# Attention with balanced column halves and inverse sums as repeated stationaries, and a recurrence with whole turnings and products over 128 stacked rows

## What is computed

```python
# attention, per block of 128 queries and head (q and k of 96, v of 64 columns)
s = einsum('bqhd,bkhd->bhqk', q_blk, k) * scale         # masked above the diagonal
o = einsum('bhqk,bkhd->bqhd', softmax(s), v)
# recurrence, per token and head (state S of 64 x 64)
sa = einsum('bhvk,bhk->bhv', S, -kk_t)
S = S * w_t + sa (x) (kk_t * a_t) + v_t (x) k_t
y = einsum('bhvk,bhk->bhv', S, r_t)
```

## Time and profile before

| | us |
|---|---|
| median of 3 runs | 1356.23 (1355.48 to 1357.2) |
| the profiled execution | 1353.33 |
| its span | 1351.5 |
| TensorE busy in the span | 1315.0 (97%) |

### The profile page before, as it was taken

One profiled execution on the slowest core, in us unless ns is written; L12 is line 12 of the kernel. 1 busy time (PEld: TensorE's weight loads), 2 busy tenths in 40 slices (PEclk: granted clock), 3 DMA queues, 4 the chain that ended last, 5 costly groups with the idle time before them and its releaser, 6 DMA issues.

```text
span 1351.5 us, 23894 instructions
## 1 busy us (share of the span) xinstructions
PE 1315.0 (97%) x9900; PEld 1071.2 (79%) x9900; DVE 945.5 (70%) x1110; ACT 474.8 (35%) x796; POOL 497.0 (37%) x323
## 2 busy tenths in 40 slices
PE   7999999999999989989999999999999999999997
PEld 6877677877776789986688878888888888888886
DVE  3657975257777634439677988877777787669877
ACT  3143643146555433334104522212222444333330
POOL 0000112001876210002084778766774354444030
PEclk9999999999999999999999999999999999999999
DMA  5111444779639952224222345444436986666562
GB/s 225 62 48 32 141 157 156 184 169 292 183 101 288 221 127 53 59 64 140 87 101 94 117 137 198 142 147 164 156 125 226 356 288 219 190 198 200 190 205 106
DMA packets 147372, 214.50 MB, mean 159 GB/s; under 512 B 79960, under 2 KB 86240, under 8 KB 146624
## 3 DMA queue, kind: packets, MB, share of 16 engines
q1 hardware_dynamic: 146976, 211.92, 49.3%
q10 hardware_dynamic: 288, 1.05, 0.2%
HBM read 137.89 MB, written 66.39 MB: 151 GB/s over the span
## 4 chain that ended last, share of the span: by engine, by line
PE 49%; DVE 3%; POOL 1%; issue 1%; ACT 1%; DVEq 0%; POOLq 0%; ACTq 0%
PE banks L2523 23%; PE banks L2410 18%; PE banks L2326 5%; PE banks L2398 2%; POOL tile_h L3083 1%; PE banks L2371 1%; DVE wout_lo L2736 0%; POOL tile_s L3083 0%; DVE y_all L2756 0%; DVE first_relu L2870 0%; PE banks L2352 0%; DVE gn_scale L2747 0%; PE banks L156 0%; PE banks L2337 0%; DVE yr_full L2762 0%
## 5 line engine op out<-in xcount | busy, mean ns | idle before, releaser
L2523 PE MATMUL banks<-stage_b_hi,stage_a_hi 128*128 128x512 f32 x448 | 174.3, 389 | 0.0
L2523 PE MATMUL banks<-stage_b_lo,stage_a_hi 128*128 128x512 f32 x448 | 174.3, 389 | 0.0
L2523 PE MATMUL banks<-stage_b_hi,stage_a_lo 128*128 128x512 f32 x448 | 174.3, 389 | 0.0
L2898 DVE TENSOR_TENSOR stage_a_lo<-stage_a_raw,stage_a_hi 128x1024 fp32r<-128x1024 f32 x56 | 97.7, 1745 | 35.2 <-ACT stage_a_hi L2665 35.2
L2665 ACT ACTIVATE stage_a_hi<-stage_a_raw 128x1024 fp32r<-128x1024 f32 x56 | 59.4, 1061 | 120.9 <-DMA stage_b_raw<-in_w_ffn 98.4
L2523 PEld LDWEIGHTS banks<-stage_b_lo,stage_a_hi 128*128 128x128 f32 x448 | 84.1, 188 | 17.6
L2523 PEld LDWEIGHTS banks<-stage_b_hi,stage_a_hi 128*128 128x128 f32 x448 | 84.1, 188 | 17.4
L2523 PEld LDWEIGHTS banks<-stage_b_hi,stage_a_lo 128*128 128x128 f32 x448 | 84.1, 188 | 17.3
L852 POOL TENSOR_TENSOR hT<-hT,rate 128x1024 f32<-128x1024 f32 x4 | 13.5, 3370 | 210.1 <-DVE kk_tile L773 210.1
L428 PE MATMUL banks<-xT_hi,win_hi 128*128 128x512 f32 x288 | 90.6, 396 | 0.0
L428 PE MATMUL banks<-xT_lo,win_hi 128*128 128x512 f32 x288 | 88.8, 389 | 0.0
(11 more groups left out here) (423 smaller groups left out, 3590.1 us busy)
## 6 DMA issues: line engine op xcount, KB each, us to landing
stage_b_raw<-in_w_ffn SPq DMA_DIRECT2D x50, 512.0 KB, 5.0
stage_a_raw<-hid_s SPq DMA_DIRECT2D x32, 512.0 KB, 4.0
w_landed<-in_w_ffn SPq DMA_DIRECT2D x30, 512.0 KB, 4.7
hid_s<-tile_s SPq DMA_DIRECT2D x60, 256.0 KB, 4.4
stage_a_raw<-hid_h SPq DMA_DIRECT2D x24, 512.0 KB, 4.0
hid_h<-tile_h SPq DMA_DIRECT2D x42, 256.0 KB, 2.0
win_raw<-in_w_in SPq DMA_DIRECT2D x20, 512.0 KB, 3.6
x_tok<-in_x SPq DMA_DIRECT2D x8, 512.0 KB, 7.6
```

The lines of the kernel that those rows point to most:

```text
L2523: last = nc.tensor.matmul(ps[:, bank, :], s[a][:, j, tok], s[b][:, j, :], start=p == 0 and j == 0 and n == 0, stop=p == NP - 1 and j == 1 ...
L2898: V.tensor_tensor(s["a_lo"][:], s["a_raw"][:], s["a_hi"][:].bitcast(F32), ALU.subtract).then_inc(lo2, 1)
```

## The change

In the attention, the two column halves take blocks (0, 3) and (1, 2) of a group in place of (0, 1) and (2, 3). The reciprocals themselves become the stationary, repeated 64 times, and the identity is what moves, so that the diagonal matrices and the two VectorE instructions that made them are gone; the sum of two row sums is a reduce with one input. The results of a column half no longer lie side by side, and SyncE moves a head's result in eight transfers in place of four.

In the recurrence, k and beta of a chunk stand beside each other (`kb`) and are turned by whole 128x128 transposes, one for each tile. v and u stand above each other (`vu`: v in partitions 0 to 63, u in 64 to 127), and so do the two score matrices of y (`rb`). The products with v and with u become one product over 128 rows. The part of `rhs` that needs no state is a step of its own (`base_step`), made at the end of the stage before, and VectorE adds it to the part with the state. The state's part of y is added likewise (`y_sum`). Three products write to other corners than before: both heads of a pair go to the same 64 columns, in two banks. `beta` is no longer loaded at once, but with one more transfer for each chunk.

```diff
@@ attention @@
-    k.quarters = lambda x, rows, tile, c: x[rows, tile, :].rearrange("p (a c j) -> p a c j", a=2, c=2)[:, :, c, :]
+    k.halves_of = ((0, 3), (1, 2))
+    k.quarters = lambda x, rows, tile, c: x[rows, tile, :].rearrange("p (a t q) -> p a t q", a=2, t=4)\
+        [:, :, k.halves_of[c][0]:k.halves_of[c][1] + 1:k.halves_of[c][1] - k.halves_of[c][0], :]
...
                 for c in range(2):
                     for dst, src in ((ym_hi, k.att_hi), (ym_lo, k.att_lo)):
-                        sp.dma_start(k.quarters(dst, rows, h // 2, c).bitcast(F32),
-                                     src[64 * c:64 * c + 64, :].rearrange("p (a j) -> p a j", a=2).bitcast(F32))\
-                            .then_inc(y_moved, 16)
+                        for a in range(2):
+                            part = src[64 * c:64 * c + 64, 2 * P * a:2 * P * (a + 1)].rearrange("p (t q) -> p t q", t=2)
+                            sp.dma_start(k.quarters(dst, rows, h // 2, c)[:, a, :, :].bitcast(F32), part.bitcast(F32))\
+                                .then_inc(y_moved, 16)
...
-                if h >= 5:
+                if h == 5:
                     sp.wait_ge(s_done, NU * (h + 1))
-                    dst, src = ((k.cum_all, k.cum_d), (k.beta_all, k.beta_d))[h - 5]
-                    sp.dma_start(dst[:], src).then_inc(reloaded, 16)
+                    sp.dma_start(k.cum_all[:], k.cum_d).then_inc(cum_in, 16)
...
+                    for c, (near, far) in enumerate(k.halves_of):
+                        near, far = base + near - at, base + far - at
+                        out = ps[64 * c:64 * c + 64, BANK_Y + g, 0:2 * P]
+                        if kt <= near + at:
+                            last = mm(out.rearrange("p (t q) -> p t q", t=2), v_all[:, kt, h, :],
+                                      src.rearrange("p (t q) -> p t q", q=P)[:, near:far + 1:far - near, :],
+                                      start=kt == 0, stop=False)
+                        elif kt <= far + at:
+                            last = mm(out[:, P:2 * P], v_all[:, kt, h, :], src[:, far * P:(far + 1) * P],
+                                      start=False, stop=kt == far + at)
...
-                for c in range(2):
-                    last = mm(ps[64 * c:64 * c + 64, BANK_Y + g, 2 * P:4 * P], ones[:, 0:HD],
-                              inverse_diag[c][:].rearrange("p j q -> p (j q)"), start=True, stop=True)
+                for j in range(2):
+                    for c in range(2):
+                        last = mm(ps[64 * c:64 * c + 64, BANK_Y + g, (2 + j) * P:(3 + j) * P],
+                                  inverse[:, of + k.halves_of[c][j]:of + k.halves_of[c][j] + 1].to_broadcast([P, HD]),
+                                  ident[:], start=True, stop=True)
...
-                    step.mark(V.tensor_tensor(total[:], sums[:, 0, of], sums[:, 1, of], ALU.add))
+                    step.mark(V.reduce_sum(total[:], sums[:, :, of].rearrange("p m q -> p q m"), AX_X))
...
-                for c in range(2):
-                    pair = inverse[:, of][:, 2 * c:2 * c + 2].rearrange("p (j o) -> p j o", o=1).to_broadcast([P, 2, P])
-                    square = ident[:].rearrange("p (o q) -> p o q", o=1).to_broadcast([P, 2, P])
-                    last = V.tensor_tensor(inverse_diag[c][:], square, pair, ALU.mult)
-                last.then_inc(inverse_ready[g], 1)
+                V.reciprocal(inverse[:, of], row_sums).then_inc(inverse_ready[g], 1)
@@ recurrence, SyncE @@
                 if m == 3:
+                    sp.wait_ge(y_mm, 1)
                     for n in range(1, 4):
                         values(n)
...
+                if m >= 2:
+                    sp.wait_ge(tr_done, m - 1)
+                sp.dma_start(kb[m % 2][:, :, B, :], k.beta_d[:, :, now(m)]).then_inc(beta_in[m % 2], 16)
@@ recurrence, TensorE @@
+            def base_step(n):
+                q = n % 2
                 pe.wait_ge(sc_ready, n + 1)
                 pe.wait_ge(v_ready, n + 1)
-                pe.wait_ge(state_ready, n + 1)
-                if n >= 1:
-                    pe.wait_ge(y_out, n)
                 for c in range(RT):
                     for p in range(2):
-                        mm(ps[own[p], B_RY, cols(c)], ks[q][own[p], c, A_, :], v_tok[q][own[p], c, :],
-                           start=True, stop=False)
+                        last = mm(ps[own[p], B_SC, cols(c)], ka[q][key_rows, p, c, :], vu[q][key_rows, p, c, :],
+                                  start=True, stop=True)
...
+            def rhs_step(n):
+                q = n % 2
+                pe.wait_ge(state_ready, n + 1)
+                for c in range(RT):
                     for p in range(2):
-                        last = mm(ps[own[p], B_RY, cols(c)], kk_all[own[p], c, now(n)], state[q][own[p], c, :],
-                                  start=False, stop=True)
+                        last = mm(ps[own[p], B_ST, cols(A0 + c)], kk_all[own[p], c, now(n)], state[q][own[p], c, :],
+                                  start=True, stop=True)
...
-                        last = mm(ps[own[p], B_SA, cols(c)], inv_t[n % 3][own[p], c, :], rhs[own[p], c, :],
+                        last = mm(ps[beta_rows, B_VU + p, cols(c)], inv_t[n % 3][own[p], c, :], rhs[own[p], c, :],
...
-                        mm(ps[own[p], B_SA, cols(c)], bk_tok[q][own[p], K, c, :], v_tok[q][own[p], c, :],
-                           start=True, stop=False)
-                    for p in range(2):
-                        last = mm(ps[own[p], B_SA, cols(c)], bk_tok[q][own[p], B, c, :], u[own[p], c, :],
-                                  start=False, stop=True)
+                        last = mm(ps[own[p], B_ST, cols(c)], kb_tok[q][:, c, p, :], vu[q][:, p, c, :],
+                                  start=True, stop=True)
...
             def y_step(n):
+                if n >= 1:
+                    pe.wait_ge(y_out, n)
...
+                        mm(ps[own[p], B_RY, cols(c)], vu[q][:, p, c, :], rb[q][:, p, c, :], start=True, stop=True)
+                if n < NC_ - 1:
+                    pe.wait_ge(v_ready, n + 2)
...
+                        last = mm(ps[own[p], B_VU, cols(Y0 + c)], state[q][own[p], c, :], rd_of(n)[own[p], c, :],
+                                  start=True, stop=True)
...
             def scores_step(m):
                 if m >= 1:
                     pe.wait_ge(kd_ready, m)
+                    pe.wait_ge(beta_in[q], 16 * ((m + 1) // 2))
                     pe.wait_ge(rd_ready, m)
                     pe.wait_ge(sc_ready, m)
+                    pe.wait_ge(base_ready, m)
...
-                        mm(ps[own[p], B_KS, cols(2 * c + R)], kd[q][own[p], c, :], rd[a][own[p], c, :],
+                        mm(ps[key_rows, B_SC + p, cols(c)], kb[q][own[p], c, K, :], rd_of(m)[own[p], c, :],
...
-                        last = mm(ps[own[p], B_B, cols(c)], beta[own[p], c, now(m)], rd[a][own[p], c, :],
+                        last = mm(ps[beta_rows, B_SC + p, cols(c)], kb[q][own[p], c, B, :], rd_of(m)[own[p], c, :],
...
+                    last = nc.tensor.transpose(ps[:, B_KB, c * P:(c + 1) * P],
+                                               kb[q][:, c, :, :].rearrange("p a n -> p (a n)"), ident[:])
@@ recurrence, VectorE @@
-                V.tensor_copy(rhs[:], view(B_RY)).then_inc(rhs_ready, 1)
+                V.tensor_tensor(rhs[:], base[:], view(B_ST, at=A0), ALU.add).then_inc(rhs_ready, 1)
...
+            def y_sum(n):
+                dve.wait_ge(part_ready, n + 1)
+                V.tensor_tensor(y_all[:, :, now(n)], y_part[:], view(B_RY), ALU.add).then_inc(y_out, 1)
```

174 lines of the change are left out of this document (90 added, 84 removed).

## The result

The changed kernel takes 1335.73 us, median of 4 runs (1334.76 to 1336.89), beside 1355.86 us for the kernel before on the same chip: a ratio of 0.9859, with an interval from 0.9844 to 0.9874. That is 20 us less. I had forecast 1342 us, with a range of 1329 to 1352.

The account below looks back on a forecast made before the run. TensorE's own time was taken to bound both parts, SyncE's moves the attention's end. Recurrence -11.7 and attention -2 took the profiled 1353.3 to 1339.6 us; with 2.9 for the median, 1342 was forecast, range 1329 to 1352.

Parts of the forecast that it names:

- attention (the barrier): End of attention: SyncE's last moves set it, so TensorE's 14 us become idle time and only 2 us are gained.
- twelve stages: Steady recurrence stages: 192 passes, four transposes and shape changes make 6.50 us each, 1.24 us less for each stage.
- from sa of chunk 15 to the end: Last chunk's chain: loses a wait of 0.6 us; wider u copy and extra sum cost what fewer passes give.
- the price of a pass: Recurrence stage: each 64-column pass takes 29.4 ns, two corners at a time; 192 passes make 5.64 us.
- rival (2): Recurrence scores: 48 passes run four at a time, 14.7 ns each, stage 0.7 us shorter, 1334 us; chance 0.12.
- The three changes of shape: Recurrence stage: TensorE goes between 64x64, whole and half array three times, 0.14 us each, 0.42 in all.
- Rival (3): Recurrence stages: SyncE or array shape changes hold each at 7.0 us or more, 1350 us; chance 0.15.
- Chunk 1's scores: Recurrence start: they wait for beta, the eighth transfer, 2.7 us late, partly swallowed by later waits; taken as 2.0.
- Chunk 3's `first_product`: Recurrence start: chunk 3's matrices, loaded behind the y wait, values and gate, come at 496.6 against 492.8, 3.8 us late.
- The clock: Recurrence start: the long wait for chunk 3's matrices can slow the clock, 1.7 us; a cold start costs nothing.
- an earlier start of SyncE's big loads: Attention's end: the 2 MB loads start sooner, 0 to 4 us left after extra moves; taken as 3.
- Rival (4): Recurrence: paired products writing the same 64 columns run one after the other, stage 8.9 us, 1378 us; chance 0.03.

Follow-up runs that it names:

- e5: Changed kernel with the scores' eight beta products in a loop of their own behind the sixteen with k; ratio up by 0.0021, 2.8 us.
- e7: Changed kernel with the four whole turnings placed one by one between small products, six more shape changes a chunk; ratio up by 0.0060, 8.1 us.
- e3: Changed kernel with the loads of values and gate spread behind those of chunks 3 to 6; by the ratio 1 us less, profiled execution 1330.0 us.
- e12: Changed kernel with later cum_all, first loads on ScalarE's queue, values and gate spread, chunk 1's beta and exponentials earlier; 1327.22 us, ratio 0.9801.
- e2: Changed kernel with neighbouring column halves (0, 1) and (2, 3) again, four moves a head instead of eight; 3.9 us less by the ratios.
- e9: Changed kernel with cum_all behind head 5's moves and its exponentials late, plus neighbouring halves with four moves a head; its time is that of e1.
- e6: Changed kernel with k and beta turned by sixteen 64x64 products instead of four whole turnings, evicted in two operations; 11.8 us slower than the changed kernel.
- e1: Changed kernel with cum_all loaded behind head 5's moves and ScalarE's exponentials at the end of its attention; ratio lower by 0.0037, 5 us.
- e11: Changed kernel with later cum_all, first loads on ScalarE's queue and neighbouring halves, four moves; 6.4 us slower than the same with balanced halves.
- e8: Changed kernel with a two-input sum and a one-input reduction added on VectorE before each of head 5's maxima; recurrence length 2.1 us off, time not given.

## Why the prediction was right, and where it wasn't

The direction and its causes were right. The size was too small: 14 us forecast, 20 measured, and the two traces, whose spans are 16.7 us apart (they are single executions), put it like this.

```
us, changed less before          forecast   traces
attention (the barrier)          -2         -0.4
start of the recurrence          +3.8       +2.3    three stages, two waits, the clock
twelve stages                    -14.9      -19.9
from sa of chunk 15 to the end   -0.6       +1.2
```

**The stages.** I said 7.74 to 6.50 us. It came to 5.79 undisturbed and 6.28 in the mean. The step that failed is the price of a pass: 29.4 ns is right for products in two corners, but the 48 passes of the scores take 20 ns each, since neighbours in the list now write the other half of the rows (0.35 us a stage hangs on that order, e5), and where `sa`, `rhs` and the state's part of y end, another 0.3 us is saved in the same way (from the trace; no run changed it). That was rival (2), and I gave it 0.12 because no row of before showed four corners at work; none could, for the old order never offered such neighbours. The three changes of shape were priced nearly right (0.14 each against 0.157, e7), with some luck: in the earlier trace rows the 0.14 were for going there and back. Against this stands a term that I didn't have at all, 0.5 us a stage, more than half of it in four stops for instructions. It took back 5.9 us in twelve stages, so the forecast came nearer to the measured time than its stages deserved. Rival (3), that SyncE's seventh load holds the stage, didn't come: no `first_product` after chunk 3's waits for its matrices.

**The start.** Chunk 1's scores waited 2.07 us for beta; I had said 2.0. Chunk 3's `first_product` waited 5.99 where I had said 3.8. The mechanism was the one named (the wait for y, values and gate, ahead of six matrices), and its size was off by issuing (5.5 us, not 5.0), landing (3.8 us after the last issue, not 3.1) and a product that was due 0.6 us sooner. The clock failed as a term: I took 1.7 us and wrote that a cold start costs nothing since the first stages wait anyway. The granted clock is 0.50 to 0.53 from 470 to 474, from 479 to 482 and from 498 to 502 (1.2 GHz), each time behind a wait; before the change it was 1.00 there throughout. TensorE was busy in nearly all of these 11 us, so they cost about 5. On the other side, the kernel before had lost 1.16 us ahead of chunk 1's scores and 1.45 us inside a step at 488, which I had not counted as its own; that one ended 1.52 us after a fetch and is a stop for instructions too.

**The end.** The last chunk's chain got 1.2 us longer, not 0.6 shorter. The clock did that. It fell to 1.2 GHz for the last three steps:

```profile
584.30:587.60 3.30, 3.03 (x48) 2.75 (x48) 0.85 (x2) 0.08 (x2) 0.00 (x0) 0.50 0.01 2
```

In e3, e5 and e12, whose clock stayed at 1.00 there, the stretch from the last `sa` to the first product behind the recurrence takes 4.43 us, the changed kernel 5.70, and the kernel before 4.54. So without the clock the chain would be 0.1 us shorter, where I had said 0.6. Ahead of the fall TensorE had a stop of 0.75 us and two waits of 0.8 and 1.0; e5 has the like and kept its clock, so what decides it isn't shown.

**The attention.** What I said of TensorE came true: `pv`'s second part is 0.43 to 0.52 us shorter (0.43 forecast), the waits for diagonals and the slow stretch are gone, and it stands idle for 9.6 us ahead of the barrier with SyncE's moves last. I kept 2 us for an earlier start of SyncE's big loads, and 0.4 came: GpSimd began with head 6 at 458.60, as before (458.63). e2 shows that TensorE can end 3.4 us later and the part still 1.1 sooner, once SyncE has four moves less, and e9 that even a beginning 6 us sooner is largely lost again in the recurrence.

What stays open: whether the traffic of beta's loads is what delays the fetches of instructions in the steady stages, and how much of e3's gain is real. Rival (4), products to the same columns one after the other, is out: no undisturbed stage comes near 8.9 us. The products over 128 stacked rows were not split again in an experiment, so their part of the gain wasn't measured by itself.

## What to carry to other kernels

Count the corners of the array that neighbouring products in the list use, not only the products: alternating row and column halves took 48 small passes from 29 to 20 ns each, and the order alone decides it. Where small products are as dense as here, the number of TensorE's instructions is a cost of its own: a turning that took the same array time in 32 passes instead of 4 cost 12 us. And before shortening an engine that ends in a barrier, look at whose last transfer ends it: here TensorE was done 9 us before the part was, and eight DMAs where four had been took 2.5 us more of the queue that did end it.

## What the hardware showed that I had not expected

- TensorE can run out of instructions in straight code: at 30 ns for a weight load and a product it stopped in every third stage (the changed kernel) or nearly every one (e6), for 0.5 to 1.9 us, and for up to 2.9 us behind three loads of 512 KB (e1, e9, e11). Each of the 69 stops in the recurrences of all kernels ended 1.2 to 1.6 us after a fetch of 16 KB had. Its busy share was as low as 71 of 80 us (e6), with hardly anything on the list of waits but "issue".
- A slower order of the same instructions (e5, +0.35 us in each stage) made the stage no slower in the mean of one profiled execution, the fastest of its five: 6.20 us against 6.28.
- A change of the array's shape costs 0.157 us (e7).
- A wait of 3 us for one load cost more than 3 us: in e9 the granted clock was 1.00 until it fell within that wait, and 0.50 to 0.53 for some 9 us behind it.
- A VectorE operation on 4 numbers with two inputs in SBUF that begins while GpSimd is at work ends 0.02 us after the GpSimd operation does, waiting up to 0.9 us (e8) or 3.6.
- SyncE's issue of a DMA took 0.61 to 0.66 us for most moves of 64 KB, and 1.5 and 3.2 us for two of the moves right behind the stores of 512 KB (e1: eight moves in 8.5 us instead of 5.2).
